# A residual stream kept token-major, with each norm made tile by tile

## What is computed

```
first block, per layer:
    x = layernorm(ALPHA * x + mixer(x), ln_mix_g, ln_mix_b)
    x = layernorm(ALPHA * x + sqrelu_mlp(x), ln_ffn_g, ln_ffn_b)
second block, per layer:
    h = rmsnorm(x, norm_mix);  x = x + mixer(h)
    h = rmsnorm(x, norm_ffn);  x = x + swiglu(h)
out = rmsnorm(x, final_norm)
```

## Time and profile before

| | us |
|---|---|
| median of 3 runs | 2824.64 (2821.25 to 2825.21) |
| span of the profiled execution | 2821.5 |
| TensorE matmuls busy (PE) | 2653.6, 94% of the span |
| VectorE busy (DVE) | 1315.1, 47% |
| GpSimd busy (POOL) | 946.3, 34% |
| ScalarE busy (ACT) | 874.4, 31% |
| granted TensorE clock, mean | 0.968 of 2.4 GHz |

### The profile page before, as it was taken

One profiled execution on the slowest core, in us unless ns is written; L12 is line 12 of the kernel. 1 busy time (PEld: TensorE's weight loads), 2 busy tenths in 40 slices (PEclk: granted clock), 3 DMA queues, 4 the chain that ended last, 5 costly groups with the idle time before them and its releaser, 6 DMA issues.

```text
span 2821.5 us, 33069 instructions
## 1 busy us (share of the span) xinstructions
PE 2653.6 (94%) x12449; PEld 2143.7 (76%) x12449; DVE 1315.1 (47%) x2055; ACT 874.4 (31%) x1185; POOL 946.3 (34%) x209
## 2 busy tenths in 40 slices
PE   8997999998888699999899899999999999899998
PEld 6565888876676488887677678888889888688886
DVE  4556533457666643445454543333641341533344
ACT  4333322223334332323432432222332322322222
POOL 3111443432222044443132234343333333244442
PEclk9999999999999899999899999999999999899999
DMA  5111223221111023222112122323323222133222
GB/s 146 53 34 45 90 89 104 89 89 60 60 60 45 30 90 97 96 91 89 45 60 75 67 75 95 99 89 104 102 80 96 73 77 75 46 104 101 92 92 72
DMA packets 168798, 224.13 MB, mean 79 GB/s; under 512 B 11806, under 2 KB 145156, under 8 KB 168588
## 3 DMA queue, kind: packets, MB, share of 16 engines
q1 hardware_dynamic: 168716, 223.00, 24.5%
HBM read 220.88 MB, written 2.10 MB: 79 GB/s over the span
## 4 chain that ended last, share of the span: by engine, by line
issue 66%; PE 16%; POOL 14%; DVE 2%; SPq 1%; ACT 0%; POOLq 0%; DMA 0%; DVEq 0%; ACTq 0%
POOL w_lo L486 14%; PE bank L515 5%; PE bank L517 5%; PE bank L516 5%; PE bank L764 1%; PE bank L761 1%; SPq L324 0%; DVE work L1768 0%; PE bank L621 0%; POOLq L496 0%; DVE work L1573 0%; DVE x_residual L1631 0%; DMA work<-in_positions 0%; ACT work L1501 0%; DVE work L1553 0%
## 5 line engine op out<-in xcount | busy, mean ns | idle before, releaser
L486 POOL TENSOR_TENSOR w_lo<-w_raw,w_hi 128x2048 fp32r<-128x2048 f32 (+1 forms) x205 | 946.1, 4615 | 1846.3 <-ACT w_hi L1146 1846.3
L515 PE MATMUL bank<-h_hi,w_hi 128*128 128x512 f32 x1568 | 620.9, 396 | 16.5 <-POOL w_lo L486 11.3
L517 PE MATMUL bank<-h_hi,w_lo 128*128 128x512 f32 x1568 | 614.2, 392 | 0.0
L516 PE MATMUL bank<-h_lo,w_hi 128*128 128x512 f32 x1568 | 614.2, 392 | 0.0
L1146 ACT ACTIVATE w_hi<-w_raw 128x2048 fp32r<-128x2048 f32 (+1 forms) x205 | 391.9, 1912 | 561.8 <-PE bank L517 556.9
L1631 DVE TENSOR_TENSOR x_residual<-x_residual,bank 128x512 f32<-128x512 f32 x560 | 380.6, 686 | 387.0 <-PE bank L517 383.6
L515 PE MATMUL bank<-act_hi,w_hi 128*128 128x512 f32 x1236 | 491.2, 397 | 25.9 <-DVE x_residual L1631 19.0
L516 PE MATMUL bank<-act_lo,w_hi 128*128 128x512 f32 x1236 | 486.7, 394 | 0.0
L517 PE MATMUL bank<-act_hi,w_lo 128*128 128x512 f32 x1236 | 485.8, 393 | 0.0
L515 PEld LDWEIGHTS bank<-h_hi,w_hi 128*128 128x128 f32 x1568 | 297.1, 190 | 87.7 <-issue 13.3
L516 PEld LDWEIGHTS bank<-h_lo,w_hi 128*128 128x128 f32 x1568 | 296.9, 189 | 63.1 <-issue 1.9
(11 more groups left out here) (220 smaller groups left out, 2218.3 us busy)
## 6 DMA issues: line engine op xcount, KB each, us to landing
w_raw<-in_ffn_w_in SPq DMA_DIRECT2D x44, 1024.0 KB, 5.1
w_raw<-in_ffn_w_up SPq DMA_DIRECT2D x32, 1024.0 KB, 5.5
w_raw<-in_ffn_w_down SPq DMA_DIRECT2D x32, 1024.0 KB, 5.1
w_raw<-in_ret_w_in SPq DMA_DIRECT2D x24, 1024.0 KB, 5.2
w_raw<-in_ffn_w_out SPq DMA_DIRECT2D x22, 1024.0 KB, 5.1
w_raw<-in_diff_w_qkv SPq DMA_DIRECT2D x12, 1024.0 KB, 5.1
w_raw<-in_fox_w_in SPq DMA_DIRECT2D x12, 1024.0 KB, 5.3
w_raw<-in_ret_w_out SPq DMA_DIRECT2D x8, 1024.0 KB, 5.0
```

The source lines that it names most:

```text
L486: nc.gpsimd.tensor_tensor(m.w_lo[:, sl, 0:width], m.w_raw[:, sl, 0:width], m.w_hi[:, sl, 0:width].bitcast(F32), ALU.subtract).then_inc(s(" ...
L515: mm(out, hi, x[0][:, k, :], start=k == 0, stop=False)
L516: mm(out, hi, x[1][:, k, :], start=False, stop=False)
L517: last = mm(out, lo, x[0][:, k, :], start=False, stop=k == kc - 1)
```

## The change

The residual becomes token-major: `m.x` is [128 tokens, 4 tiles, 1024 features]. Output projections go through `pe_tokens` with the activations stationary and 512 weight columns streamed, so block n is half n%2 of token tile n//2 (in retention tile n%4 of half n//4). The last group of a stage uses all eight banks (`LAST_BANKS`). The sums of a norm run along the free axis, tile by tile; gains and shifts are loaded as rows on all partitions. Normed tiles are turned to the feature-major h in two halves of 256 tokens, and `pe_input` makes the first two blocks of the next stage on the first half while the second is made. The rms factor is in h, so all later multiplies by `m.rb` and `rcol` go (MLA's latents keep theirs). Fox logits are made by `pe_tokens` with 8 columns. SP issues the row loads between weight loads, behind waits for the norm before. The cores of the diff, cut:

```diff
+LAST_BANKS = (4, 5, 6, 7, 0, 1, 2, 3)
-    m.x = sb("x_residual", [P, KC, T])
+    m.x = sb("x_residual", [P, TT, D])
...
+def pe_input(m, pe, t, made, source, added, count, unit):
+    for half in range(2):
+        pe.wait_ge(*m.upto(made, 2 * half + 2))
+        if half:
+            pe.wait_ge(*m.upto(f"{t}_h_lo", 4))
+        for j in range(4):
+            for k in (2 * j, 2 * j + 1):
+                for tile in (2 * half, 2 * half + 1):
+                    at = 256 * (k % 2) + P * (tile % 2)
+                    last = nc.tensor.transpose(b[4 + j][:, at:at + P], source(tile)[:, k * P:(k + 1) * P], m.ident)
+            last.then_inc(s(f"{t}_h_turned"), 1)
+        pe_weights(m, pe, [unit])
+        pe.wait_ge(*m.upto(added, count - 2))
+        w, cols = weight(m, [unit], 2048, KC), slice(256 * half, 256 * half + 256)
+        for j in range(2):
+            for k in range(KC):
+                if j == 0 and k % 2 == 0:
+                    pe.wait_ge(*m.upto(f"{t}_h_hi", 4 * half + k // 2 + 1))
+                    pe.wait_ge(*m.upto(f"{t}_h_lo", 4 * half + k // 2 + 1))
...
+                last = mm(b[j][:, cols], lo, m.h_hi[:, k, cols], start=False, stop=k == KC - 1)
...
 def pe_relu_mlp / pe_swiglu down, pe_pairs output, pe_retention output
-            pe_features(m, b[4 + n % 4][:, :], weight(m, names, 2048, 2), n * P,
-                        (m.act_hi[:, at:at + 2, :], m.act_lo[:, at:at + 2, :]), 2)
+            pe_tokens(m, b[banks[n % len(banks)]][:, :], weight(m, names, 2048, 2),
+                      (m.act_hi[:, at:at + 2, :], m.act_lo[:, at:at + 2, :]), 2, n // 2, 512, 512 * (n % 2))\
...
+def act_high(m, act, t, half):
+    for j in range(4):
+        act.wait_ge(*m.upto(f"{t}_h_turned", 4 * half + j + 1))
+        m.nc.scalar.activation(m.h_hi[:, 2 * j:2 * j + 2, 256 * half:256 * half + 256],
+                               m.bank[4 + j][:, :].rearrange("p (k t) -> p k t", k=2), ACT.Copy).then_inc(m.sem(f"{t}_h_hi"), 1)
+def act_std(m, act, t, tile, eps, bias=0.0):
+    run(m.squares, m.x[:, tile, :], ACT.Square, bias=bias, accum_out=m.x_sq[:, tile:tile + 1]).then_inc(s(f"{t}_sq"), 1)
+    act.wait_ge(*m.upto(f"{t}_sq", tile + 1))
+    run(m.x_std[:, tile:tile + 1], m.x_sq[:, tile:tile + 1], ACT.Sqrt, scale=1 / D, bias=m.eps[:, eps:eps + 1])...
+act_layernorm:
+    deviation(0), deviation(1), scale(0), scale(1), deviation(2)
+    act_high(m, act, to, 0)
+    deviation(3)
+    act_split(m, act, [second])
+    scale(2), scale(3)
+    act_high(m, act, to, 1)
+act_rms:
+    scale(0), scale(1), scale(2)
+    act_high(m, act, t, 0)
+    scale(3)
+    act_split(m, act, [second])
+    act_high(m, act, t, 1)
...
 dve_add_block
+    if sums:
+        v.scalar_tensor_tensor(out=x, in0=x, scalar=1.0, in1=bank[:, :], op0=ALU.mult, op1=ALU.add,
+                               accum_out=m.x_sum[:, n:n + 1]).then_inc(s(f"{t}_acc"), 1)
+dve_low: h_lo = bank - h_hi, four pieces of 128x512 per half
+dve_rms_tile: reciprocal of one column, then
+    v.scalar_tensor_tensor(out=out, in0=m.x[:, tile, :], scalar=m.x_rstd[:, tile:tile + 1], in1=m.gain_2[:, :], op0=ALU.mult, op1=ALU.mult)
+dve_layernorm, center(tile):
+        add(2 * tile), add(2 * tile + 1)
+        v.tensor_scalar(mean, m.x_sum[:, at[0]], m.x_sum[:, at[1]], -1.0 / D, ALU.add, ALU.mult)
+        v.scalar_tensor_tensor(out=m.centered[:, tile % 2, :], in0=m.x[:, tile, :], scalar=mean, in1=m.gain, op0=ALU.add, op1=ALU.mult)
+    finish(tile): reciprocal of one column, then
+        v.scalar_tensor_tensor(out=m.x[:, tile, :], in0=m.centered[:, tile % 2, :], scalar=m.x_rstd[:, tile:tile + 1], in1=m.shift,
+                               op0=ALU.mult, op1=ALU.add)
+    center(0), center(1), finish(0), finish(1), scale(0), scale(1), center(2)
+    dve_low(m, dve, to, 0)
+    center(3), finish(2), finish(3), scale(2), scale(3)
+    dve_low(m, dve, to, 1)
+dve_rms:
+    add(0), add(1), scale(0), scale(1), add(2)
+    dve_low(m, dve, t, 0)
+    add(3), scale(2), scale(3)
+    dve_low(m, dve, t, 1)
+dve_end:
+    add(0), add(1), scale(0), add(2), scale(1), add(3), scale(2), scale(3)
...
 sp_program
+    def layernorm_rows(which, layer):
+        sp.dma_start(m.gain, d[f"ln_{which}_g"][layer:layer + 1, :].broadcast_to([P, D])).then_inc(s("ln_rows_in"), 16)
+        sp.dma_start(m.shift, d[f"ln_{which}_b"][layer:layer + 1, :].broadcast_to([P, D])).then_inc(s("ln_rows_in"), 16)
+    def beside_diff():
+        sp.wait_ge(*m.upto("ln1_done", TT))
+        layernorm_rows("mix", 1)
+    def beside_sw0():
+        sp.wait_ge(*m.upto("sw0_normed", TT))
+        rms_row(d["norm_mix_2"][1:2, :])
+        sp.dma_start(m.ret_angles, d["c_angles"]).then_inc(s("ret_tables_in"), 16)
...
 pe_fox_gates
-        pe_features(m, b[2][:, :], (m.wf_hi, m.wf_lo), 0, (m.h_hi, m.h_lo), KC, done="fox_logits")
+            last = pe_tokens(m, b[2][:, 8 * t:8 * t + 8], (m.wf_hi, m.wf_lo), (m.h_hi, m.h_lo), KC, t, 8)
```

More of the change, by code:

```diff
@@ L810, in step @@
             attention(0), scores(1)
-        if project:
-            queries(1), gates[0]()
+        if project and (not first or t == "mla"):
+            queries(1)
         head_sums(0)
         if project:
-            keys(1), gates[1]()
+            keys(1)
             if t == "mla":
@@ L1250, in act_pairs, with act_rms, scale, row_by_row @@
+def act_rms(m, act, t, added, count, per_tile, second):
+    def scale(tile):
+        act.wait_ge(*m.upto(added, count + per_tile(tile)))
+        act_std(m, act, t, tile, 1)
+    scale(0), scale(1), scale(2)
[3 more added lines that the diff above has]
+    act_high(m, act, t, 1)
+def row_by_row(tile):
+    return 2 * tile + 2
+def half_by_half(tile):
+    return TT + tile + 1
 def act_pairs(m, act, t):
@@ L1713, in dve_pairs, with dve_low @@
-def dve_pairs(m, dve, t, then):
+    if sums:
+        v.scalar_tensor_tensor(out=x, in0=x, scalar=1.0, in1=bank[:, :], op0=ALU.mult, op1=ALU.add,
+                               accum_out=m.x_sum[:, n:n + 1]).then_inc(s(f"{t}_acc"), 1)
+    elif first and t in POST_NORMED:
+        v.scalar_tensor_tensor(out=x, in0=x, scalar=ALPHA, in1=bank[:, :], op0=ALU.mult, op1=ALU.add).then_inc(s(f"{t}_acc"), 1)
+    else:
+        v.tensor_tensor(x, x, bank[:, :], ALU.add).then_inc(s(f"{t}_acc"), 1)
+def dve_low(m, dve, t, half):
+    for j in range(4):
+        dve.wait_ge(*m.upto(f"{t}_h_hi", 4 * half + j + 1))
+        hi, lo = (h[:, 2 * j:2 * j + 2, 256 * half:256 * half + 256] for h in (m.h_hi, m.h_lo))
+        m.nc.vector.tensor_tensor(lo, m.bank[4 + j][:, :].rearrange("p (k t) -> p k t", k=2), hi.bitcast(F32), ALU.subtract)\
+            .then_inc(m.sem(f"{t}_h_lo"), 1)
@@ new lines, in dve_rms_tile @@
+def dve_rms_tile(m, dve, t, tile, out, rows):
+    s, v = m.sem, m.nc.vector
+    dve.wait_ge(*m.upto(f"{t}_std", tile + 1))
+    v.reciprocal(m.x_rstd[:, tile:tile + 1], m.x_std[:, tile:tile + 1]).then_inc(s(f"{t}_rstd"), 1)
+    dve.wait_ge(*m.upto(f"{t}_rstd", tile + 1))
+    if tile == 0:
+        dve.wait_ge(*m.upto("gain_in", 16 * rows))
+    if tile == 2 and t != "out":
+        dve.wait_ge(*m.upto(f"{t}_h_turned", 4))
+    v.scalar_tensor_tensor(out=out, in0=m.x[:, tile, :], scalar=m.x_rstd[:, tile:tile + 1], in1=m.gain_2[:, :], op0=ALU.mult, op1=ALU.mult)\
+        .then_inc(s(f"{t}_normed"), 1)
@@ L1714, in dve_pairs, with dve_rms, scale @@
+def dve_rms(m, dve, add, t, rows):
+    def scale(tile):
+        dve_rms_tile(m, dve, t, tile, m.normed[:, tile % 2, :], rows)
+    add(0), add(1), scale(0), scale(1), add(2)
+    dve_low(m, dve, t, 0)
+    add(3), scale(2), scale(3)
+    dve_low(m, dve, t, 1)
+POST_NORMED = ("mla", "ffn0", "diff", "ffn1")
+def dve_pairs(m, dve, t, end):
     s, b, v = m.sem, m.bank, m.nc.vector
@@ L1830, in step @@
             dve.wait_ge(*m.upto("lat_rows", 2))
-        if project and not (t == "fox" and ps[0] == 0):
+        if project and ps[0] == 0 and t == "diff":
+            take("q", 0), take("q", 1), take("k", 0)
+        elif project and not (t == "fox" and ps[0] == 0):
             take("q", 0), take("k", 0)
@@ L1839, in step @@
         head_rstd(0)
-        if project and not (t == "fox" and ps[0] == 0):
+        if project and not (t != "mla" and ps[0] == 0):
             take("q", 1)
@@ L1930, in dve_lambda, with dve_relu_mlp @@
     dve.wait_ge(*m.upto("lam_steps", 3))
-def dve_relu_mlp(m, dve, t, norm, then):
+def dve_relu_mlp(m, dve, t, norm, end):
     s, b, v = m.sem, m.bank, m.nc.vector
@@ L2006, in dve_swiglu, with dve_retention @@
             gs = range(2 + e, G2 - 1, 2)
[L2007 to L2012 removed]
+            up(gs, i), down(range(1 + e, G2 - 2, 2), i)
+    up([G2 - 1]), down([G2 - 2])
+    end(adder([G2 - 1]))
+def dve_retention(m, dve, end):
     s, b, v = m.sem, m.bank, m.nc.vector
@@ L2088, in step @@
             else:
-                dve_last_blocks(m, dve, add, "ret", KC * (RH - 1), then)
+                for n in range(TT):
+                    add(n)
+                end(lambda tile: add(TT + tile))
```

(11 more changed lines are left out.)

575 lines of the change are left out of this document (235 added, 340 removed).

## The result

The changed kernel takes **2753.6 us** as the median of four runs (2752.5 to 2754.4), against 2824.9 for the kernel before on the same chip: a ratio of 0.9748, 95% interval 0.9734 to 0.9762. The profiled execution has a span of 2750.7 us, 2.9 under the median, so the two profiled spans differ by 70.8 us, and these can be placed stretch by stretch.

The account below looks back on a forecast made before the run. TensorE, busy 94% of the 2821.5 us span, was taken as the bound, with gains only where it stands still. Terms summed to -34.1 us, span 2787.4, plus 3.1 for the median: 2790.5 us; range 2764 to 2816.

Parts of the forecast that it names:

- The clock term: At each new norm boundary, TensorE's gaps bring the 1.2 GHz level: 4 us each, bounds 0 and 15.2.
- the overlap is better: Rival: gaps short enough that the clock costs 0 to 1 us per boundary, 25 us more won, 2766; chance 0.2.
- The chains without the clock: Steps from last output block through first new products: layernorms 20.5, 23.3, 20.5, about 33 us; rms 16.9 plus second unit's 10.9.
- a 1024-wide centring or multiply: VectorE's per-tile norm steps reading SBUF twice: 1.34 us each, bounds 0.75 and that plus a 4.6 us POOL split.
- h_hi behind tile 2's square: Layernorms: ScalarE may start h_hi only behind tile 2's square, 3.0 us after the last block.
- centring held by POOL's split: Second layernorm: POOL's split, 8.6 to 4.0 us before the end, holds tile 0's centring and pushes all by 2.8 us.
- The copy: A 128x512 VectorE copy took 3.62 us beside POOL's split, 0.42 with POOL idle; read as evidence for VectorE-POOL blocking.
- Fox logits: Fox gates: 96 products of 8 columns at 0.11 us, 10.6 us, replace 5.5 and 2.5 us: +2.6 us.
- The last wait for banks: Retention's last half no longer waits for banks: -2.4 us.
- Diff: Diff's first values wait 1.3 us for POOL; q parts come first and the split starts earlier: -1.3 us.
- SP's waits: SP waits for a norm's end before loading gains, shifts, next weights: 0 taken; cover gone, 5 us at three boundaries.
- tail: Behind the last product, transposes, table load and most of eight multiplies go: 6.8 us in place of 15.6, -8.8.

Follow-up runs that it names:

- gap filled: Changed kernel plus 16 unread matmuls of 256 columns in TensorE's wait between the first half's turns and its products; 2757.6 us, ratio 0.9769 to the kernel before.
- one pass: Changed kernel, but both halves of h are turned first and the first two blocks' products run once, 512 columns wide; 2795.3 us, ratio 0.9909 to the kernel before.
- split early: Changed kernel with ScalarE's high part of the next weights ahead of tile 3's square in the four layernorms; 2772.7 us, ratio 0.9814 to the kernel before.
- split in two: Changed kernel with each POOL split as two instructions of 128x1024 in place of one of 128x2048; 2743.4 us, ratio 0.9717 to the kernel before.

## Why the prediction was wrong, and where it was right

**The clock term failed.** It was 4 us at each of seven boundaries, 28 us; measured is 1.0 us, at the fourth. That is 27 of the 37 us that were missed. Two things were wrong in it. First its source: the earlier trace rows shows 6.3 us of slow products behind one wait of 5.8 us, on a chain where nothing could take them up. The new waits were 2.5 us at most in the first three layernorms and 0.6 us at most in the rms norms, and the 2.4 us before the first products follow from the prediction's own times (turns end at 1.9, products start at 4.5). Only the fourth layernorm had waits of the size that the term was taken from (5.6 and 6.6 us). Second and worse, its place in the sum: the text lets the first half end at 10.3 and tile 3 be ready at 12.4, which is 2.1 us of slack (1.3 measured), and then adds the whole clock cost to the end of the chain. By its own steps a first half 1.5 us slower costs nothing, which "gap filled" showed. The rival "the overlap is better" had the size right (clock costs 0 to 1 us, 2766 us) and the reason in part: the gaps were short enough at four boundaries; at the second and third the clock did fall, and slack hid it.

The Trainium skill's rule, "TensorE: Matmul & The Clock Gate", section on HAM oscillation, that products between waits fall back to the slow clock each time, holds in "one pass", where behind waits of 5.5 to 14.8 us no boundary's clock is above 0.92, and in "split early". In the changed kernel four boundaries have all products at full clock, the second and third hide the loss, and the fourth hides it in its first half and pays 1.0 us in the turns of its second.

**The chains without the clock were right.** Predicted 20.5, 23.3, 20.5 and 33 to 33.5 us, measured 19.6, 22.3, 19.5 and 33.2; rms 27.8 with the second unit, measured 27.3, 27.4 and 26.7. Together these make 5 us more of gain, and 6 if the 1.0 us of clock in the fourth is taken out. Steps, term by term: a 1024-wide centring or multiply 1.28 us (1.34 taken); h_hi behind tile 2's square at 2.85 (3.0); first products at 4.3 (4.5); the sum's read on VectorE 0.08 us (0 taken, bound 0.2); centring held by POOL's split from 8.6 us before the end, 2.8 us; the fourth's multiply held 3.3 us.

The Trainium skill, "SBUF — State Buffer", section "Who interferes with whom", says that such a pair excludes each other for a whole instruction. "Split early" (5.00 us) and "split in two" (1.83) agree: the hold ends with POOL's instruction. The other way round fits too: in the first layernorm POOL's split started 0.6 us before the end of VectorE's last multiply and took 5.08 us instead of 4.6. The copy, which the prediction read as agreeing, has one SBUF input and is another case than this pair. VectorE's h_lo, with one input in PSUM, kept its 0.62 us a piece beside a split.

**Fox logits were mis-sized.** 96 x 0.11 = 10.6 us was taken from 20 such matmuls, and they took 18.3: a row of 2.2 us can't show what 18 us of them do to the clock. Fox as a stage: +7.8 instead of +2.6.

**Retention and diff.** The last wait for banks went, as said (-2.4), and with it the slow clock around it. In the kernel before, the matmuls ahead of that wait and behind it:

```profile
2407.90:2426.40 18.50, 18.46 (x72) 14.79 (x72) 4.14 (x3) 5.25 (x6) 7.90 (x2) 0.89 0.18 57
...
2428.85:2436.00 7.15, 7.15 (x25) 5.76 (x26) 5.74 (x9) 6.20 (x10) 0.00 (x0) 0.76 0.46 147
```

After, the same 96 matmuls stand in one piece:

```profile
2357.71:2379.66 21.95, 21.95 (x97) 18.09 (x98) 7.68 (x11) 6.74 (x9) 9.22 (x2) 1.00 0.15 49
```

28.1 us became 21.9, a gain of 6.2, of which 2.4 is the wait and the rest the clock. It isn't safe: three later kernels had this piece at 23.3 to 23.8. Diff won 3.3 us where 1.3 were counted; the other 2.0, and 1.6 and 1.4 in the two swiglus, I haven't traced.

**Right:** loops at 0; nothing late behind SP's waits; start -1.3 (-1.5); tail 7.0 against 6.8. The sum of misses is 27 (clock) + 6 (chains) + 4 (retention) + 2 (diff) + 3 (swiglus) - 5 (logits) = 37 us.

## What to carry to other kernels

When a cost is added to a chain, say on which of its branches it falls: a slow first half is free if another engine sets the second, and its slack stands in the same sum; a slow second half is not. Handing over half of the tokens was worth some 45 of 71 us here, because the half that waits and the half that works are on different engines; order the other engines' instructions so that a weight split doesn't meet a two-input VectorE instruction on that chain, or cut the split. Price a spell of short matmuls from a spell as long, and read PEclk beside the busy share.
